# Compression of keys and values in four column groups of TensorE, with a late copy of the last chunk

## The reference

```
def compress(kr, pe, w1, w2):      # kr (256, 4, 64); w1 (32, 64, 256); w2 (256, 64); pe (32, 64)
    chunks = kr.reshape(b, t // 16, 16, 4, 64)            # 16 chunks of 16 tokens
    lo = einsum("bclgd,ldh->bcgh", chunks, w1[:16])
    hi = einsum("bclgd,ldh->bcgh", chunks, w1[16:])
    h = lo[:, :-1] + hi[:, 1:] + einsum("ld,ldh->h", pe, w1)   # window n = chunk n and chunk n + 1
    return einsum("bngh,hd->bngd", silu(h), w2)
```

## Time and profile before

| | |
|---|---|
| median of the runs | 749.98 us |
| the profiled execution, its own time | 750.86 us |
| its span, first to last instruction | 749.1 us |
| TensorE busy (matmuls) | 726.7 us, 97% |
| VectorE, ScalarE, GpSimdE busy | 514.0, 368.9, 70.7 us |
| mean granted TensorE clock | 0.991 of full speed |
| the chain that ended last | PE 89%, DVE 6%, ACT 3% |

### The profile page before, as it was taken

How to read it: one execution, slowest core, us unless ns; L and a number is a source line. 1 busy time by engine, 2 the same in 40 slices (tenths; PEclk the granted TensorE clock), 3 DMA queues, 4 the chain that set the end, 5 groups by cost and what they waited for, 6 DMA issues and landing times.

```text
span 749.1 us, 13432 instructions
## 1 busy us (share of the span) xinstructions
PE 726.7 (97%) x5817; PEld 693.2 (93%) x5817; DVE 514.0 (69%) x614; ACT 368.9 (49%) x508; POOL 70.7 (9%) x72
## 2 busy tenths in 40 slices
PE   5899999999999999999999999999999999999996
PEld 4899999999999999999999999887899999998884
DVE  4998688777665777764446898897885756555361
ACT  3454444452645445543435575478854644444341
POOL 1500111003000000000003200000000232231001
PEclk9799999999999999999999999999999999999999
DMA  9989856877625577685654570704165665564611
GB/s 343 377 288 350 282 184 213 283 262 241 210 73 168 180 247 255 220 281 176 215 174 121 169 225 1 225 1 159 35 218 193 212 201 193 173 223 144 215 36 56
DMA packets 118335, 146.49 MB, mean 196 GB/s; under 512 B 4004, under 2 KB 103556, under 8 KB 118276
## 3 DMA queue, kind: packets, MB, share of 16 engines
q1 hardware_dynamic: 116912, 143.58, 58.1%
q10 hardware_dynamic: 1364, 2.05, 0.8%
HBM read 144.57 MB, written 1.05 MB: 194 GB/s over the span
## 4 chain that ended last, share of the span: by engine, by line
PE 89%; DVE 6%; ACT 3%; DMA 1%; issue 1%; POOLq 0%; SPq 0%; DVEq 0%; ACTq 0%
PE bank L602 68%; PE bank L1113 8%; PE bank L784 3%; DVE mod_acc L1547 2%; DMA raw<-in_w_ada 1%; PE bank L927 1%; PE bank L662 1%; PE bank L639 1%; PE bank L890 1%; PE bank L888 1%; PE bank L868 1%; PE bank L964 1%; DVE w_lo L1560 1%; PE bank L907 1%; ACT score L1417 1%
## 5 line engine op out<-in xcount | busy, mean ns | idle before, releaser
L1560 DVE TENSOR_TENSOR w_lo<-raw,w_hi 128x2048 fp32r<-128x2048 f32 x108 | 244.8, 2271 | 114.8 <-ACT w_hi L1157 114.6
L1157 ACT ACTIVATE w_hi<-raw 128x2048 fp32r<-128x2048 f32 x108 | 204.7, 1899 | 212.7 <-PE bank L602 159.8
L602 PE MATMUL bank<-act_hi,w_hi 128*128 128x256 f32 x816 | 228.2, 282 | 0.5 <-ACT act_hi L1314 0.2
L602 PE MATMUL bank<-act_lo,w_hi 128*128 128x256 f32 x816 | 226.2, 279 | 0.8 <-DVE act_lo L1619 0.5
L602 PE MATMUL bank<-act_hi,w_lo 128*128 128x256 f32 x816 | 222.2, 279 | 0.0
L602 PEld LDWEIGHTS bank<-act_hi,w_hi 128*128 128x128 f32 x816 | 154.3, 189 | 3.6 <-issue 3.1
L602 PEld LDWEIGHTS bank<-act_lo,w_hi 128*128 128x128 f32 x816 | 153.4, 188 | 1.7 <-DVE act_lo L1619 0.7
L602 PEld LDWEIGHTS bank<-act_hi,w_lo 128*128 128x128 f32 x816 | 151.0, 188 | 0.0
L602 PE MATMUL bank<-ffn_hi,w_hi 128*128 128x256 f32 x352 | 98.0, 278 | 0.0
L602 PE MATMUL bank<-ffn_hi,w_lo 128*128 128x256 f32 x352 | 97.3, 277 | 0.4 <-DVE w_lo L1560 0.4
L602 PE MATMUL bank<-ffn_lo,w_hi 128*128 128x256 f32 x352 | 97.2, 276 | 0.0
(11 more groups left out here) (285 smaller groups left out, 1059.5 us busy)
## 6 DMA issues: line engine op xcount, KB each, us to landing
raw<-in_w_in SPq DMA_DIRECT2D x31, 1024.0 KB, 6.4
raw<-in_w_ada SPq DMA_DIRECT2D x24, 1024.0 KB, 6.8
raw<-in_w_gate_up SPq DMA_DIRECT2D x22, 1024.0 KB, 5.1
raw<-in_w_mlp_in SPq DMA_DIRECT2D x16, 1024.0 KB, 5.4
raw<-in_w_mlp_out SPq DMA_DIRECT2D x16, 1024.0 KB, 5.2
raw<-in_w_down SPq DMA_DIRECT2D x10, 1024.0 KB, 5.0
raw<-in_w_out SPq DMA_DIRECT2D x8, 1024.0 KB, 7.1
raw<-in_w_proj_conv SPq DMA_DIRECT2D x2, 1024.0 KB, 5.5
```

The lines of the kernel that those rows point to most:

```text
L602: i = e.matmul(dst, lhs, rhs, start=start and k == 0 and (m == 0 or second is not None) and n == 0, stop=stop and k == kt - 1 and n == 2, ...
L1157: e.activation(w_hi[slot][:, 0:kt * n_cols], raw[i % N_RAW][:, 0:kt * n_cols], ACT.Copy).then_inc(hi_split, 1)
L1560: e.tensor_tensor(w_lo[slot][:, 0:kt * n_cols], raw[i % N_RAW][:, 0:kt * n_cols], w_hi[slot][:, 0:kt * n_cols].bitcast(F32), ALU.subtract) ...
```

## The change

Four edits, all of them around `compress`:

1. The stationary window is 64 columns (4 heads by 16 chunks, less one), cut into two sets of 32. Each of the 8 tiles is now two matmuls of 32 stationary columns, and the output rows (0, 32, 64 or 96) depend on the set and on whether the tile is even or odd: `to = (j % 2 * 2 + s_) * SET`. A half is 16 matmuls in place of 8. Even and odd tiles are summed in different rows.
2. `cmp_hidden` multiplies `cmp_out` (now 128 rows) with `ident_2`, a 128 x 64 tile that is two identities one above the other, in place of the transposes: it turns the sums and adds the rows of even and odd tiles. GpSimdE makes `ident_2` in place of clearing the fifth group.
3. There is no fifth group. The embedding's two parts stand in columns 63 and 64, and column 63 is the place of the last chunk of the last head, which half 0 doesn't need.
4. Half 1 needs the last chunk there. `last_chunk` copies it, 64 rows by 8 elements on VectorE and as much on ScalarE, after half 0 has read the column. Half 1 now waits for both copies.

```diff
-        N_WINDOWS = (KV + 1) * N_CHUNKS - 1
+        SET = 2 * N_CHUNKS
+        LAST_CHUNK = KV * N_CHUNKS - 1
-            cmp_in = alloc(own, "cmp_in", [P, CMP_LEN // 4, KV + 1, N_CHUNKS])
+            cmp_in = alloc(own, "cmp_in", [P, CMP_LEN // 4, KV * N_CHUNKS + 2])
+            ident_2 = alloc(own, "ident_2", [P, HD])
...
             def compress(name):
+                pe.wait_ge(cmp_paired_dve, second * (KV + 2) + KV + 1 + half)
+                pe.wait_ge(cmp_paired_act, second * (KV + 1) + KV + half)
                 if half == 0:
-                    pe.wait_ge(cmp_paired_dve, KV + 1 if not second else 2 * (KV + 1))
-                    pe.wait_ge(cmp_paired_act, KV if not second else 2 * KV)
...
                 for j in range(CHUNK_TILES):
-                    flat_in = cmp_in[:, j].rearrange("p g c -> p (g c)")
-                    t = e.matmul(bank[SUMS][0:N_WINDOWS, 0:CMP_HID], flat_in[:, half:half + N_WINDOWS], src[:, j, :],
-                                 start=(half == 0 and j == 0), stop=(half == 1 and j == CHUNK_TILES - 1),
-                                 skip_group_check=True)
+                    for s_ in range(2):
+                        at, to = half + s_ * SET, (j % 2 * 2 + s_) * SET
+                        t = e.matmul(bank[SUMS][to:to + SET, 0:CMP_HID], cmp_in[:, j, at:at + SET], src[:, j, :],
+                                     start=(half == 0 and j < 2), stop=(half == 1 and j >= CHUNK_TILES - 2),
+                                     skip_group_check=True)
                 t.then_inc(compressed, 1)
             def cmp_hidden(which):
...
                 for m in range(2):
-                    t = e.transpose(b[:, m * P:m * P + N_WINDOWS], cmp_out[:, m * P:(m + 1) * P],
-                                    ident[0:N_WINDOWS, 0:N_WINDOWS])
+                    t = e.matmul(b[:, m * P:m * P + HD], cmp_out[:, m * P:(m + 1) * P], ident_2[:], start=True, stop=True,
+                                 skip_group_check=True)
...
+            def last_chunk(which):
+                act.wait_ge(compressed, 2 * which + 1)
+                src = cmp_raw[HD:2 * HD, 1, :].rearrange("p (c l two) -> p two l c", two=2, l=STRIDE // 2)
+                e.activation(cmp_in[HD:2 * HD, :, LAST_CHUNK:LAST_CHUNK + 1], src[:, 1, :, N_CHUNKS - 1:],
+                             ACT.Copy).then_inc(cmp_paired_act, 1)
...
             for h in range(QH + 3):
                 head(h)
+                if h - 1 in (in2_heads.index("w1k0"), in2_heads.index("w1v0")):
+                    last_chunk(int(h - 1 == in2_heads.index("w1v0")))
...
+            def last_chunk(which):
+                dve.wait_ge(compressed, 2 * which + 1)
+                src = cmp_raw[HD:2 * HD, 1, :].rearrange("p (c l two) -> p two l c", two=2, l=STRIDE // 2)
+                e.tensor_copy(cmp_in[0:HD, :, LAST_CHUNK:LAST_CHUNK + 1], src[:, 0, :, N_CHUNKS - 1:]).then_inc(
+                    cmp_paired_dve, 1)
...
                 if 1 <= h <= QH:
                     normalise(h - 1)
+                if h - 1 in (in2_heads.index("w1k0"), in2_heads.index("w1v0")):
+                    last_chunk(int(h - 1 == in2_heads.index("w1v0")))
```

More of the change, by code:

```diff
@@ L172, in build @@
         KC_AT = (C_HEADS - 1) * N_CMP
-        N_WINDOWS = (KV + 1) * N_CHUNKS - 1
+        SET = 2 * N_CHUNKS
+        LAST_CHUNK = KV * N_CHUNKS - 1
+        assert 4 * SET == P and KV * N_CHUNKS == HD
         IN_FLIGHT = 3
@@ L216, in build @@
         pc_T = wide[1][0:C_ROWS, 5:7, :]
-        cmp_out = wide[1][0:N_WINDOWS, 7, :]
+        cmp_out = wide[1][:, 7, :]
         mean = conv_tmp[:, 0, :]
@@ L934, in cmp_hidden @@
                 pe.wait_ge(cmp_copied, which + 1)
+                pe.wait_ge(tables_pool, ROWS_SET)
                 for m in range(2):
-                    t = e.transpose(b[:, m * P:m * P + N_WINDOWS], cmp_out[:, m * P:(m + 1) * P],
-                                    ident[0:N_WINDOWS, 0:N_WINDOWS])
+                    t = e.matmul(b[:, m * P:m * P + HD], cmp_out[:, m * P:(m + 1) * P], ident_2[:], start=True, stop=True,
+                                 skip_group_check=True)
                 t.then_inc(cmp_turned, 1)
@@ L1322, in compress_copy @@
                     act.wait_ge(cmp_turned, 1)
-                e.activation(cmp_out, bank[SUMS][0:N_WINDOWS, 0:CMP_HID], ACT.Copy).then_inc(cmp_copied, 1)
+                e.activation(cmp_out, bank[SUMS][:, 0:CMP_HID], ACT.Copy).then_inc(cmp_copied, 1)
             def cmp_hidden(which):
@@ L1343, in pair_tokens @@
                         "p (c l two) -> p two l c", two=2, l=STRIDE // 2)
-                    e.activation(cmp_in[HD:2 * HD, :, g, :], src[:, 1], ACT.Copy).then_inc(cmp_paired_act, 1)
+                    n = N_CHUNKS - (g == KV - 1)
+                    e.activation(cmp_in[HD:2 * HD, :, g * N_CHUNKS:g * N_CHUNKS + n], src[:, 1, :, 0:n],
+                                 ACT.Copy).then_inc(cmp_paired_act, 1)
[3 more added lines that the diff above has]
+                e.activation(cmp_in[HD:2 * HD, :, LAST_CHUNK:LAST_CHUNK + 1], src[:, 1, :, N_CHUNKS - 1:],
+                             ACT.Copy).then_inc(cmp_paired_act, 1)
             def evacuate(name):
@@ L1895, in pair_tokens @@
                         "p (c l two) -> p two l c", two=2, l=STRIDE // 2)
-                    e.tensor_copy(cmp_in[0:HD, :, g, :], src[:, 0]).then_inc(cmp_paired_dve, 1)
-                e.tensor_copy(cmp_in[:, :, KV, 0:2], cols(f"cmp_{name[0]}_pe_2", 0, CMP_LEN // 2).rearrange(
+                    n = N_CHUNKS - (g == KV - 1)
+                    e.tensor_copy(cmp_in[0:HD, :, g * N_CHUNKS:g * N_CHUNKS + n], src[:, 0, :, 0:n]).then_inc(cmp_paired_dve, 1)
+                e.tensor_copy(cmp_in[:, :, LAST_CHUNK:LAST_CHUNK + 2], cols(f"cmp_{name[0]}_pe_2", 0, CMP_LEN // 2).rearrange(
                     "p (s l) -> p l s", s=2)).then_inc(cmp_paired_dve, 1)
+            def last_chunk(which):
[3 more added lines that the diff above has]
+                    cmp_paired_dve, 1)
             def evacuate(name):
@@ L1931, in evacuate @@
                     if which:
-                        dve.wait_ge(cmp_paired_act, KV)
-                        dve.wait_ge(cmp_paired_dve, KV)
+                        dve.wait_ge(cmp_paired_act, KV + 1)
+                        dve.wait_ge(cmp_paired_dve, KV + 2)
                     e.tensor_tensor(cmp_raw, src, rstd_2, ALU.mult).then_inc(cmp_scaled, 1)
@@ L1972, in cmp_pe_copy @@
                     dve.wait_ge(kc_made, 1)
-                e.tensor_copy(cmp_pe[:], src[:, :, KV, 0]).then_inc(cmp_pe_set, 1)
+                e.tensor_copy(cmp_pe[:], src[:, :, KV - 1, N_CHUNKS - 1]).then_inc(cmp_pe_set, 1)
             def conv_mean():
@@ L2238, in gpsimd_program @@
             e.memset(own_rows[:], 1.0).then_inc(tables_pool, 1)
-            e.memset(cmp_in[:, :, KV, :], 0.0).then_inc(tables_pool, 1)
+            e.tensor_tensor(ident_2[:], ident[:, 0:HD], ident[:, HD:], ALU.add).then_inc(tables_pool, 1)
             pool.wait_ge(mod_summed, 6)
```

## The result

| | before | changed |
|---|---|---|
| median of 20 runs each, us | 749.74 | 755.75 |
| ratio, 95% interval | | 1.0074, 1.005 to 1.0099 |
| profiled execution, its own time, us | 750.86 | 755.28 |
| its span, us | 749.1 | 753.6 |
| mean granted clock | 0.991 | 0.981 |

A forecast was written before the change was run, and what follows sets the result against it. TensorE was taken to bound the kernel, holding 89% of the chain. Turn 4's -0.5, turn 9's +3.3 and the clock's +2.7 gave +5.5 us, 755.5 us on the median; 8-in-10 range 750.0 to 759.5.

The forecast's parts named there:

- Part 1, the matmuls: Halves in `compress`: four groups run four abreast, 1.8 us a half instead of 3.65, gaining 1.85 us.
- The exit: Way out of the column groups behind each half 1, before the transposes: 0.2 us.
- the way in: Issue time before the groups, 0.33 us at `attend`; not counted before half 1, where TensorE waits anyway.
- Part 2, the keys: Turn 4: half 1 waits 2.7 us for the late copies, yet 0.5 us is gained.
- part 4: Clock: turn 9's wait brings half speed from 514.8 to 525.0, costing 2.7 us; no fall counted in turn 4.
- I count no fall there and keep it as a rival: Turn 4: the 2.7 us wait, hardly longer than 2.45, adds no clock loss; rival that it does, chance 0.15.
- The rival's price of up to 3.5 us: Clock fall in turn 4: half speed for some 7 us, up to 3.5 us lost, total 758.5; chance 0.15.
- Part 3, the values: Turn 9: TensorE waits 6.6 us for ScalarE's copy behind head 9's exponentials; second scores 2.8 us later.
- The sign "the transposes of head 8 at 521": Behind half 1 of the values: transposes of head 8 start at 521 in place of 517.42.
- Part 5: Rest put at nothing: `cmp_hidden` some 0.2 us more, covered by a wait; small copies and GpSimdE's sum off the path.
- the +2.8 of turns 4 and 9: Sum of turn 4's -0.5 us and turn 9's +3.3 us, before the clock's cost.
- the rival on the other side: Faster: ScalarE's values copy ends by 512.3, keys' gain of 1.85 x 2 stays, 746.3 us; chance 0.10 with related cases.

The follow-up runs named there:

- experiment 3: Changed kernel plus 10 and 26 dummy identity matmuls before half 1 of keys and values, copies still late: 752.32 us, ratio 1.0039 to the kernel before.
- experiment 2: Changed kernel with only the values' late copies moved ahead in their queues, to turn 8: 753.23 us, ratio 1.0045 to the kernel before.
- experiment 4: Changed kernel with late copies, but 8 matmuls of 64 stationary columns a half, no groups: 758.52 us, ratio 1.0120 to the kernel before.
- experiment 1: Changed kernel with both late copies, keys' and values', moved ahead in the VectorE and ScalarE queues: 750.43 us, ratio 1.0010 to the kernel before.
- experiment 7: Changed kernel, both copies early, groups for keys only, one convolution tap step moved later from VectorE's turn 3: 746.78 us, ratio 0.9965 to the kernel before.

## Why the prediction was right, and where it was not

The forecast was 755.5 us and the median 755.75. The total agrees better than its terms do: turn 4 took 1.7 us more than the sum has, and the rest of the kernel, put at nothing, gave 1.0 us back. That they nearly cancel is luck.

- **Part 1, the matmuls: right.** A half is 1.93 us in the timeline and 1.86 us on the chain, for 1.8. Each record stands for 1.93 / 32 = 0.060 us, against 0.228 before: 3.8 times. The Trainium skill (TensorE: Matmul & The Clock Gate, Part 3) has three column tiles at 2.38 times; by an estimate from it, 3.2 times for four, a half would take 2.3 us. The measurement decides for the sum's 1.8. The exit was put at 0.2: behind a half at full clock the transposes take 0.81 us in experiment 3, 0.15 more than the 0.66 of the earlier trace rows. The 0.33 us that the prediction takes for the way in stands before the 79-column half 0 as well (464.61 in the chain of before), so no row shows it to be the groups'. The 0.70 us of `attend` was reckoned from the start of a weight load; the chain's 1.45 us for 16 records gives 0.72 for 8, which changes nothing.
- **Part 2, the keys: the wait right, the clock wrong.** Wait 2.54 us for 2.7, released by the copies behind the instructions named. From half 0 to the product `q2`, the stretch takes 13.24 us before (464.94 to 478.18, the latter from the chain of before) and 14.48 us after (463.28 to 477.76): +1.2 us where the sum has -0.5. Half 1 takes 2.99 us and the transposes 1.38, against 1.93 and 0.81 at full clock in experiment 3: 1.6 us in all; without them the stretch stands at -0.4.
- **The step that failed is in part 4: "I count no fall there and keep it as a rival."** The fall came, in the changed kernel and in experiment 2, each time with a wait of some 2.5 us, and neither with one of 1.08 us (experiment 4) nor with the wait filled (experiment 3). "Hardly longer" than 2.45 us was no reason to leave it out of the sum, and the 2.45 us of the earlier trace rows was no delay to compare with: counted from the start of the wait, the falls came after 1.4 us (turn 9), 2.0 and 2.2 (experiment 2), 2.4 (experiment 1), 2.8 (experiment 4) and 3.3 (turn 4). The rival's price of up to 3.5 us was too high in turn, because it supposed a fall as long as that of the start: this one lasted 3.4 us and cost 1.6.
- **Part 3, the values: right.** TensorE waits 6.91 us for 6.6, for ScalarE's copy behind head 9's exponentials. From ScalarE's copy at 506.65 to the second scores at 524.54 it is 17.89 us, against 12.03 before (507.27 to 519.30): +5.9 us for 3.3 + 2.7 = 6.0. Turns 10 to 14 gave hardly any of it back: from the second scores to the product at 541.74 it is 17.2 us, and 17.5 before (519.30 to 536.76).
- **Part 4, the clock in turn 9: right, with luck in the length.** 513.5 to 523.7 for 514.8 to 525.0. At half speed were half 1 (3.64 us, for 1.93 in experiment 3) and the transposes (1.35 for 0.80): 2.3 us for 2.7. The 10.2 us were taken from a single fall. In experiment 4 the fall of turn 9 lasted 6.8 us, and so did the one at the start of experiments 3 and 7, where the kernel before has 10.2. The sign "the transposes of head 8 at 521" was reckoned at full clock, against the forecast's own fall; they began at 522.62.
- **Part 5: right.** `cmp_hidden` takes 0.30 us more, hidden behind the same wait.

The sum as a whole can be weighed against the runs. With the clock held by filling (experiment 3) the loss is 2.8 us by the medians and 2.2 by the trace behind half 0, for the +2.8 of turns 4 and 9. The clock's share is 3.4 us by the medians, for the 2.7 of the forecast; by the traces it is 1.6 + 2.3 = 3.9 us. The stretches add up to 1.2 + 5.9 = 7.1 us. The rest gave 1.0 us back: 0.20 between the two stretches, 0.26 in turns 10 to 14 and 0.55 behind 541.74. That leaves 6.1 us, and the medians have 6.0. The profiled pair has only 4.4 us, because the changed kernel's profiled execution reached half 0 of the keys 1.7 us earlier (463.28 for 464.94); over the eight experiments that moment differs by 1.5 us, and what sets it is open. So is whether every execution has the same falls: of the changed kernel's, the four with a mean clock of 0.986 to 0.988 took 754.0 to 754.6 us and the five with 0.981 took 755.3 to 756.3, but those at 0.985 lie anywhere from 754.9 to 757.9. The one that was traced had 0.981.

What would have made the change work is the rival on the other side: it needs ScalarE's copy before 512.3, and the queue has an empty place for it in turn 8. Even so it gives 750.43 and not the rival's 746.3. Of the 4.1 us between them, 1.6 are the keys', where the next limit is VectorE's scaling of head 3 (2.1 us gained for 3.7), and 2.4 come because the shorter halves leave TensorE idle for 3.07 us and the clock falls. That the values' halves are filling was read correctly from the earlier trace rows; that filling also holds the clock, and that a faster half 1 uncovers this, I had not counted in any case.

## What to carry to other kernels

Before a small copy is made a condition of a matmul, find the place in the queue of its engine, not its duration: here 0.21 us of ScalarE made TensorE wait 6.9 us, and moving the two copies up gave back 5.3 us. Work that fills a wait off the chain is not free to shorten: when it goes, the clock may go too, so put a piece of real work of the right length there, and make faster only what lies on the chain; then look for the next limit, which here was VectorE 0.8 us later. And a wait near the length that has brought the clock down before belongs in the sum, at a price, not only among the rivals.

## What the runs showed of the hardware

- Four column groups of 32 in plain float32, two records a matmul, run at 3.8 times the rate of one 64- or 79-column matmul after another. All 32 weight loads of a half fit in 1.45 us beside them:

```profile
507.41 1.45 PEld L931 LDWEIGHTS bank<-raw,cmp_in 128*32 128x32 f32 x32 [0.33 <-issue]
```

- The clock can fall after the wait is over: at 472.5, when half 1 had run since 471.8. The same stands at the start of experiment 7, where TensorE waited 4.43 us until 20.37 and the clock fell at 20.8, to return at 27.7:

```profile
20.00:21.00 1.00, 0.63 (x5) 0.64 (x6) 1.00 (x2) 0.00 (x0) 0.00 (x0) 0.92 1.01 401
...
27.00:28.00 1.00, 1.00 (x8) 1.00 (x8) 1.00 (x2) 0.91 (x3) 0.25 (x1) 0.67 1.14 364
```

- The length of the wait alone doesn't set how long the fall lasts. With waits of 2.54 and 2.53 us it was 3.4 us, with 5.18 us (experiment 4) and 4.43 us (experiment 7) 6.8 us, with 3.07, 3.76 and 6.91 us 10.2 us. What does set it stays open.
- 64x8 copies took 0.21 us on ScalarE and 0.17 us on VectorE, less than the 0.25 and about the 0.2 that I took for them.
